# Moving the gate products ahead of their table piece, and three edits beside it, in the expert stage of a two-block transformer kernel

## The reference, cut to what matters

```python
def peer_ffn(h, w_q, sub_keys, u_tab, v_tab):
    q = (hf @ w_q).reshape(T, PEER_HEADS, 2, PEER_HALF)
    s = jnp.einsum('thpd,hpnd->thpn', q, sub_keys)          # 8 heads, 2 sides, 128 keys
    sv, si = lax.top_k(s, PEER_TOPK)                        # the best 16 of each side
    cand = sv[:, :, 0, :, None] + sv[:, :, 1, None, :]
    cv, ci = lax.top_k(cand.reshape(...), PEER_TOPK)        # the best 16 of 256 sums
    expert = ...                                            # first key * 128 + second key
    g = jax.nn.softmax(cv, axis=-1)
    ...
        a = gelu(einsum('cd,chkd->chk', x_c, u_tab[e_c]))
        return einsum('chk,chkd->cd', g_c * a, v_tab[e_c])
```

## Time and profile before

| What | Value |
|---|---|
| median of 3 runs | 1623.45 us (1622.08 to 1624.24) |
| the profiled execution | 1628.74 us, its span 1626.9 us |
| mean granted clock of PE | 0.987 |
| PE busy | 1551.1 us (95%) |
| PEld busy | 1339.1 us (82%) |
| DVE busy | 1132.8 us (70%) |
| ACT busy | 812.6 us (50%) |

### The profile page before, as it was taken

One profiled execution on the slowest core, in us unless ns is written; L12 is line 12 of the kernel. 1 busy time (PEld: TensorE's weight loads), 2 busy tenths in 40 slices (PEclk: granted clock), 3 DMA queues, 4 the chain that ended last, 5 costly groups with the idle time before them and its releaser, 6 DMA issues.

```text
span 1626.9 us, 30962 instructions
## 1 busy us (share of the span) xinstructions
PE 1551.1 (95%) x10658; PEld 1339.1 (82%) x10658; DVE 1132.8 (70%) x2580; ACT 812.6 (50%) x1362; POOL 105.9 (7%) x132
## 2 busy tenths in 40 slices
PE   6999999999999989998999999999999999999997
PEld 5877877896777768776999999999998777778886
DVE  3565666646666475448469996888888999965555
ACT  3664565446457545444356665344334444445454
POOL 1030600100113100000000000000000000000000
PEclk9999999999999999989999999999999999999999
DMA  6443654666355556424544546444444444465552
GB/s 240 153 167 125 214 188 135 218 192 235 129 189 181 205 177 233 149 73 168 188 136 168 182 166 207 155 156 160 159 156 151 160 167 162 161 209 192 192 193 103
DMA packets 78215, 280.40 MB, mean 172 GB/s; under 512 B 9377, under 2 KB 11457, under 8 KB 76865
## 3 DMA queue, kind: packets, MB, share of 16 engines
q1 hardware_dynamic: 74176, 261.97, 48.0%
q0 software_dynamic: 3968, 17.52, 3.2%
HBM read 277.31 MB, written 2.14 MB: 172 GB/s over the span
## 4 chain that ended last, share of the span: by engine, by line
PE 78%; DVE 15%; ACT 3%; issue 2%; DMA 2%; POOL 0%; ACTq 0%; DVEq 0%; POOLq 0%
PE banks L714 22%; PE banks L715 21%; PE banks L716 21%; DVE w_lo L1526 5%; PE banks L1137 3%; PE banks L901 2%; PE banks L860 2%; PE banks L799 2%; PE banks L821 1%; PE banks L911 1%; PE banks L910 1%; DMA arena<-x_spill 1%; ACT w_hi L1213 1%; DVE arena L2009 1%; PE banks L909 1%
## 5 line engine op out<-in xcount | busy, mean ns | idle before, releaser
L1526 DVE TENSOR_TENSOR w_lo<-raw,w_hi 128x1024 fp32r<-128x1024 f32 x456 | 549.9, 1210 | 307.8 <-ACT w_hi L1213 303.6
L1213 ACT ACTIVATE w_hi<-raw 128x1024 fp32r<-128x1024 f32 x456 | 474.3, 1043 | 572.2 <-PE banks L716 543.8
L714 PE MATMUL banks<-w_hi,xT_hi 128*128 128x512 f32 (+2 forms) x1140 | 453.4, 398 | 17.7 <-DVE w_lo L1526 10.7
L716 PE MATMUL banks<-w_hi,xT_lo 128*128 128x512 f32 (+2 forms) x1140 | 442.6, 388 | 0.0
L715 PE MATMUL banks<-w_lo,xT_hi 128*128 128x512 f32 (+2 forms) x1140 | 442.2, 388 | 0.0
L714 PE MATMUL banks<-xT_hi,w_hi 128*128 128x256 f32 x1360 | 391.8, 288 | 4.4 <-DVE w_lo L1526 1.7
L715 PE MATMUL banks<-xT_lo,w_hi 128*128 128x256 f32 x1360 | 385.9, 284 | 0.0
L716 PE MATMUL banks<-xT_hi,w_lo 128*128 128x256 f32 x1360 | 385.7, 284 | 0.0
L714 PEld LDWEIGHTS banks<-w_hi,xT_hi 128*128 128x128 f32 x1140 | 216.7, 190 | 64.7 <-issue 8.9
L714 PEld LDWEIGHTS banks<-xT_hi,w_hi 128*128 128x128 f32 x1360 | 261.2, 192 | 5.8 <-issue 3.8
L715 PEld LDWEIGHTS banks<-xT_lo,w_hi 128*128 128x128 f32 x1360 | 261.7, 192 | 0.1
(11 more groups left out here) (204 smaller groups left out, 1345.1 us busy)
## 6 DMA issues: line engine op xcount, KB each, us to landing
raw<-stream SPq DMA_DIRECT2D x490, 512.0 KB, 3.6
arena<-ln_in POOLq DMA_DIRECT2D x4, 1024.0 KB, 6.2
arena<-x_spill POOLq DMA_DIRECT2D x3, 1024.0 KB, 10.4
arena<-mod_rows POOLq DMA_DIRECT2D x2, 1536.0 KB, 9.6
raw<-stream SPq DMA_DIRECT2D x6, 256.0 KB, 4.5
arena<-g_in POOLq DMA_DIRECT2D x3, 512.0 KB, 11.1
raw<-stream SPq DMA_DIRECT2D x8, 160.0 KB, 2.4
arena<-bands_in POOLq DMA_DIRECT2D x1, 1024.0 KB, 6.1
```

What stands on the lines that cost most here:

```text
L714: pe.matmul(out, stationary[0], moving[0], start=first, stop=False, **k)
L716: return pe.matmul(out, stationary[1], moving[0], start=False, stop=last, **k)
L1213: act.activation(part(w_hi[:, s]), part(half_raw(s)), ACT.Copy).then_inc(piece_hi, 1)
L1526: dve.tensor_tensor(part(w_lo[:, s]), part(half_raw(s)), part(w_hi[:, s].bitcast(F32)), ALU.subtract).then_inc(piece_lo, 1)
```

## The change

Five edits, all in the expert part.

1. On PE, `gates` stands ahead of the piece's product in each step of loops 2 and 3. The steps of DVE keep their order.
2. The one-hot rows of a loop's first step are made ahead of the loop: those of loop 2 ahead of DVE's wait for `a_taken`, those of loop 3 ahead of the last `gate_hidden` of loop 2. The refills of ring slot 3 at both loop ends move behind the splits of the first four rows.
3. The rows of `hidden`'s second half are split into slots 4 to 7 of `xT_hi` and `xT_lo`, which were free in loop 3, in place of slots 0 to 3.
4. The matmuls that clear banks 0 to 3 wait one by one for `a_taken`, in place of all of them for the last.
5. The scores' units take the bank pairs 0, 2, 3, 1. Each waits for its own unit of the queries, and loop 1 waits for the first unit's copies; ACT lets PE into banks 2 and 3 only when all scores are copied (`a_taken` is raised by 2, and by 2 more behind the wait).

```diff
-        E["scores"] = [Unit(plan, "own", [...] , COPY2) for j in range(4)]
+        E["scores"] = [Unit(plan, "own", [...] , COPY2,
+                            pair=(0, 2, 3, 1)[j]) for j in range(4)]
...
-            wait_put(pe, E["q"])
             pe.wait_ge(keys_loaded, 16)
             for j4, u in enumerate(E["scores"]):
+                wait_put(pe, E["q"][j4:j4 + 1])
                 bank_free(u)
...
-            def second_table(j, s):
+            def second_table(j, s, row=0):
...
-            wait_put(pe, E["scores"])
+            wait_put(pe, E["scores"][:1])
...
             with pe.Fori(0, HALF // RING) as i:
                 for s in range(RING):
+                    gates(RING * i, s)
                     first_table(RING * i + HALF, s)
-                    gates(RING * i, s)
-
-            pe.wait_ge(a_taken, NKEYS + RING)
+
             for q in range(4):
+                pe.wait_ge(a_taken, NKEYS + q + 1)
                 pe.matmul(banks[:, q], const("zeros").bitcast(BF16)[:, 0:P], kept[:, 0:2 * P].bitcast(BF16), start=True, stop=True)
             with pe.Fori(0, HALF // RING) as i:
                 for s in range(RING):
+                    gates(RING * i + HALF, s)
                     second_table(RING * i, s)
-                    gates(RING * i + HALF, s)
             with pe.Fori(0, HALF // RING - 1) as i:
                 for s in range(RING):
-                    second_table(RING * i + HALF, s)
+                    second_table(RING * i + HALF, s, RING)
...
-            act.sem_inc(a_taken, RING)
+            act.sem_inc(a_taken, 2)
+            wait_put(act, E["scores"])
+            act.sem_inc(a_taken, RING - 2)
...
-            with act.Fori(0, HALF // RING) as i:
+            with act.Fori(0, HALF // RING - 1) as i:
                 for s in range(RING):
                     gelu(RING * i + HALF, s)
-
+            for s in range(RING - 1):
+                gelu(NKEYS - RING, s)
+            act.wait_ge(piece_used, FIRST_U + NKEYS)
+            gelu_only(NKEYS - RING, RING - 1)
             act.wait_ge(g_taken, HALF + 2)
             for s in range(RING):
                 split_hidden(0, s)
+            split_piece(FIRST_U + NKEYS, RING - 1)
...
-            for s in range(RING):
+            for s in range(RING - 1):
                 refill(HALF - RING, s, True, False)
 
             act.wait_ge(g_taken, 2 * HALF + 2)
             for s in range(RING):
-                split_hidden(HALF, s)
+                split_hidden(HALF, s, RING)
+            refill(HALF - RING, RING - 1, True, False)
...
-                one_hot(half, 0, 0)
                 with dve.Fori(0, HALF // RING - 1) as i:
                     for s in range(RING):
                         step(i, s, True, rows)
-                for s in range(RING):
-                    step(HALF // RING - 1, s, s < RING - 1, False)
+                for s in range(RING - 1):
+                    step(HALF // RING - 1, s, True, False)
+                if half == 0:
+                    one_hot(1, 0, 0)
+                gate_hidden(half, HALF - RING, RING - 1)
...
+            one_hot(0, 0, 0)
             dve.wait_ge(a_taken, HALF + RING)
             gate_half(0, FIRST_U + HALF, False)
             dve.wait_ge(a_taken, NKEYS + RING)
             for s in range(RING):
                 rest_of_hidden(0, s)
+            rest_of_piece(FIRST_U + NKEYS, RING - 1)
             gate_half(1, FIRST_V, True)
             for s in range(RING):
-                rest_of_hidden(HALF, s)
+                rest_of_hidden(HALF, s, RING)
+            rest_of_piece(FIRST_V + HALF, RING - 1)
```

More of the change, by code:

```diff
@@ L428, in build @@
         E["q"] = feature_units(peer["qT"], 2 * PEER_HEADS)
-        E["scores"] = [Unit(plan, "own", [peer["scores"][:, b, 4 * j:4 * j + 4] for b in range(B)], COPY2) for j in range(4)]
+        E["scores"] = [Unit(plan, "own", [peer["scores"][:, b, 4 * j:4 * j + 4] for b in range(B)], COPY2,
+                            pair=(0, 2, 3, 1)[j]) for j in range(4)]
         E["pick"] = [Unit(plan, "turn", [picked[:, 0:2], picked[:, 2:3]], [("act", "copy"), ("dve", "three_parts")], tiles=3, pair=3)]
@@ L1146, in second_table @@
                     for d in range(D // COLS):
-                        mm = parts_product(banks[:, 2 * b + d], [x[:, s, b * P:(b + 1) * P] for x in (xT_hi, xT_lo)],
+                        mm = parts_product(banks[:, 2 * b + d], [x[:, row + s, b * P:(b + 1) * P] for x in (xT_hi, xT_lo)],
                                            [x[:, s, d * COLS:(d + 1) * COLS] for x in (w_hi, w_lo)],
@@ L1175, in _ @@
                 for s in range(RING):
+                    gates(RING * i + HALF, s)
                     second_table(RING * i, s)
-                    gates(RING * i + HALF, s)
             with pe.Fori(0, HALF // RING - 1) as i:
                 for s in range(RING):
-                    second_table(RING * i + HALF, s)
+                    second_table(RING * i + HALF, s, RING)
             def last_products(b, d, s):
-                return parts_product(banks[:, 2 * b + d], [x[:, s, b * P:(b + 1) * P] for x in (xT_hi, xT_lo)],
+                return parts_product(banks[:, 2 * b + d], [x[:, RING + s, b * P:(b + 1) * P] for x in (xT_hi, xT_lo)],
                                      [x[:, s, d * COLS:(d + 1) * COLS] for x in (w_hi, w_lo)], False, False, skip_group_check=True)
@@ L1432, in _, with gelu_only @@
                 evacuate(u)
+            def gelu_only(j, s):
+                act.activation(hidden[:, bass.ds(j + s, 1)].rearrange("p a t -> p (a t)"), banks[:, s, 0:S],
+                               ACT.Gelu).then_inc(a_taken, 1)
             def gelu(j, s):
@@ L1437, in gelu, with split_hidden, refill @@
                 split_piece(FIRST_U + j + RING, s)
[L1438 to L1445, removed]
+                gelu_only(j, s)
+            def split_hidden(j, s, row=0):
+                act.activation(xT_hi[:, row + s], hidden[:, bass.ds(j + s, 1)].rearrange("p a t -> p (a t)"), ACT.Copy).then_inc(hidden_hi, 1)
+            def refill(j, s, pieces, rows, row=0):
                 act.wait_ge(piece_used, FIRST_V + j + s + 1)
@@ L1449, in refill @@
                 if rows:
-                    split_hidden(j + RING, s)
-            act.sem_inc(a_taken, RING)
+                    split_hidden(j + RING, s, row)
+            act.sem_inc(a_taken, 2)
+            wait_put(act, E["scores"])
+            act.sem_inc(a_taken, RING - 2)
             act.wait_ge(spilled, 16)
@@ L1483, in _ @@
             for s in range(RING):
-                split_hidden(HALF, s)
+                split_hidden(HALF, s, RING)
+            refill(HALF - RING, RING - 1, True, False)
             with act.Fori(0, HALF // RING - 1) as i:
                 for s in range(RING):
-                    refill(RING * i + HALF, s, True, True)
+                    refill(RING * i + HALF, s, True, True, RING)
             root_table()
@@ L2083, in rest_of_piece, with rest_of_hidden @@
                 split_rest(s)
-            def rest_of_hidden(j, s):
+            def rest_of_hidden(j, s, row=0):
                 dve.wait_ge(hidden_hi, j + s + 1)
-                dve.tensor_tensor(xT_lo[:, s], hidden[:, bass.ds(j + s, 1)].rearrange("p a t -> p (a t)"), xT_hi[:, s].bitcast(F32),
-                                  ALU.subtract).then_inc(hidden_lo, 1)
+                dve.tensor_tensor(xT_lo[:, row + s], hidden[:, bass.ds(j + s, 1)].rearrange("p a t -> p (a t)"),
+                                  xT_hi[:, row + s].bitcast(F32), ALU.subtract).then_inc(hidden_lo, 1)
             def gate_half(half, first_piece, rows):
@@ L2120, in _ @@
                     rest_of_piece(FIRST_V + HALF + RING * i + RING, s)
-                    rest_of_hidden(RING * i + HALF + RING, s)
+                    rest_of_hidden(RING * i + HALF + RING, s, RING)
             dve.wait_ge(end_loaded, 48)
```

## The result

| | before | after |
|---|---|---|
| median | 1623.85 us (4 runs) | 1664.24 us (1663.61 to 1665.28, 4 runs) |
| profiled execution: span | 1626.9 us | 1662.7 us |
| ratio of the times | | 1.0246, 95% interval 1.0234 to 1.0258 |

A forecast was written before the change was run, and what follows sets the result against it. PE was taken to bound the kernel, 78% of the span, without waits inside loops 2 and 3. Terms 18.5 + 22.9 - 2.0 - 1.3 = +38.1 us took the median from 1623.45 to 1661.5, range 1652 to 1671.

The forecast's parts named there:

- loop 2, first gates to end of last piece: Loop 2: late one-hot rows, branches and low clock at its start make it 228.5 us, before 210.00: +18.5.
- joint and loop 3, to loop 4: From loop 2's end to loop 4's first product: 234.0 us for 211.1, with late one-hot rows: +22.9.
- clock and rest behind loop 4's start: Loop 4's start: the 2.36 us idle goes, and the low clock behind it too: -2.0.
- scores: Around the scores: the 1.18 us wait goes, with the issue around it: -1.3, bounds -2.5 and 0.
- The chain in the steps: Loops 2 and 3: gates s+2 start at least 3.71 or 4.05 us after piece s is issued, 0.38 or 0.84 late.
- the branches: Loop 2: ACT starts a piece 0.1 us later in one step of four, at its loop's branch; 1.4 us added.
- the formula: Two steps take 3.71 + 3.33 us (7.04) in loop 2 and 4.05 + 3.21 us (7.26) in loop 3.
- Loop 2's start: First gates come at the same time as before, PE idles 4.0 us ahead of them, low clock costs 2.2 us.
- The joints: Loop 3's first product at about 1.8 us, its next gates another 1.1 us late; no wait at loop 4.
- the rows are not late: Rival for loops 2 and 3: one-hot rows 0.38 and 0.84 us sooner; 1622.8, or 1615.5 with first rows; chance 0.07.
- A clock that falls in the loops: Second rival, loops 2 and 3: one step in four at half clock, +80, some 1740 us; chance 0.03.
- A price per restart: Third rival, late gates in the loops: 0.1 us for each of 62, +6, 1668 us; chance 0.16.

The follow-up runs named there:

- e1: Changed kernel with VectorE's step reordered: gate_hidden, then the one-hot rows for the gates two steps on, then rest_of_piece; 1624.7 us, ratio 0.9998.
- e5: Changed kernel with one more VectorE instruction (128x512 bf16, output unread) in each one_hot; 1686.10 us, ratio 1.0382.
- e6: Changed kernel with one more VectorE instruction (128x512 bf16, output unread) per step, between gate_hidden and rest_of_piece; 1665.29 us, ratio 1.0257.
- e3: Changed kernel with the gates behind the piece again in loop 3 alone; 1637.69 us, ratio 1.0080.
- e4: Changed kernel with the second half's rows of hidden split into slots 0 to 3 again; 1665.37 us, ratio 1.0250.
- e2: e1 plus loop 2's one-hot rows of steps 0 and 1 made right behind the picks and each half's last gate_hidden ahead of the last rest_of_piece; 1616.35 us.
- e7: Kernel before the change with one more VectorE instruction (128x512 bf16, output unread) in each one_hot; 1628.99 us, ratio 1.0030.
- e9: e2 with the gates behind the piece in loops 2 and 3, as in the kernel before; 1622.82 us, ratio 0.9983.

## Why the prediction was right, point by point

| Term | forecast | measured, from the two traces |
|---|---|---|
| loop 2, first gates to end of last piece | 228.5 against 210.00: +18.5 | 228.37: +18.4 |
| of this, low clock at the start | 2.2 | 5.50 - 3.33 = 2.2 |
| joint and loop 3, to loop 4 | 234.0 against 211.1: +22.9 | 234.58: +23.5 |
| clock and rest behind loop 4's start | -2.0 | 183.35 against 184.96: -1.6 |
| scores | -1.3 | 7.49 against 8.56: -1.1 |
| sum | +38.1 | +39.2 |

The spans differ by 35.8 us only, since the profiled execution of before had its scores at 820.87 and that of after at 817.52, ahead of all that was changed; the medians differ by 40.4. Between 39.2 and 40.4 lies 0.07% of the time, which I can't place. The forecast for the median, 1661.5, took over the 5.3 us by which the profiled execution of before was longer than its median. That step had no ground: the profiled execution of after is 0.3 us longer than its median, 1664.53 against 1664.24. So the sum of the terms was 1.1 us short, and the forecast of the median 2.7.

**The chain in the steps** held in its mechanism (e1, e5, e6) and its size: 7.04 us and 1.4 for the branches make 7.085 for a mean pair of loop 2, and 7.08 is there; in loop 3 7.26 were forecast and 7.27 are there. The branches show in loop 2 as one late step in four of 3.80 us and not 3.71. The share between the two loops held too (e3). One detail did not hold throughout: the wait was to fall on each second step. In loop 2 it does. In loop 3 it moves: steps of 3.49 and 3.78 us at 1301.05 to 1308.32, both longer than 3.21, but 3.23 and 4.14 at 1450.78 to 1458.15. By the formula a pair's sum is fixed, and its share between the two steps is free as long as neither is above 4.05, or 4.14 with a branch.

**Loop 2's start** went as worked out: the first gates came 191.39 us after loop 1's start, 191.40 before, and 3.99 us of idle stood ahead of them, with the clock low behind.

**The joints.** First product of loop 3: at 1.7 us and not 1.8 (1244.77 to 1246.45), and the gates behind its piece (2.87 us) 0.87 us late (1250.19) and not 1.1. At loop 4 I wrote that nothing is waited for; there are 0.44 us. The last `gate_hidden` stands behind a `rest_of_piece` on DVE, the same kind of dependence that I had followed in the loops and did not follow here. That joint and loop 3 together are within 0.6 us of the forecast is in part luck: the first joint was 0.3 us shorter than forecast, and loop 4's start 0.6 later. The gain was credited to two edits together; e4 shows that one of them carries none of it.

**The rivals.** That the rows are not late was given 0.07 and a condition; e1 and e2 make the condition true by another edit, and give 1624.7 and 1616.4 where it had 1622.8 and 1615.5. A clock that falls in the loops did not come: 0.99 for loop 2, whose start holds all of it, and 1.00 for loop 3 with some 9% of idle time. A price per restart is not seen: two steps take what the chain alone gives.

## What to carry to other kernels

Where one engine's queue holds both what the next step needs and what waits for this step, moving the consumer one place forward takes a whole step from the slack; here 2.96 us to spare in loop 2 (6.67 - 3.71) became 0.38 us too late. Follow the chain from the event that frees the waiting instruction to the consumer's new place, and compare it with one step. An instruction costs by where it stands in the queue and not by what it takes: the same 0.34 us of VectorE cost 22 us on the chain and about nothing beside it. When a reordering loses, look for the producer that must be moved with it; here an earlier place of the one-hot rows on VectorE, in the steps and at the loops' ends (e1, e2), turned a loss of 2.5% into a kernel 0.45% faster than the one before.

## What the runs showed of the hardware

At the joints of the expert part TensorE's granted clock was full behind idle times of 1.03, 1.12, 1.18 and 1.42 us. It went to its lower level behind those of 1.84 (e7), 1.98 and 2.26 (e9), 2.36 (before) and 3.99 us (after). I had not expected it behind 1.98. What this costs is not fixed: behind 3.99 us the first step of loop 2 took 5.50 us in the changed kernel and 4.66 in e4, for 3.33 at the full clock. Nor does the length of one idle time decide it. In the first part of the changed kernel's trace an idle of 2.07 us left the clock full, and one of 1.12 us, where PE works in short groups, was followed by the lower level:

```profile
62.99 0.47 PE L715 MATMUL banks<-w_hi,xT_hi 128*128 128x512 f32 x1 [2.07 <-DVE xT_lo L1571]
...
60.00:66.00 6.00, 3.93 (x22) 3.23 (x21) 3.78 (x7) 3.00 (x7) 0.00 (x0) 1.00 0.54 177
...
693.53 1.46 PE L861 MATMUL banks<-arena 64*128 64x128 f32 x4 [1.12 <-issue]
...
693.70:700.50 6.80, 6.80 (x22) 5.11 (x22) 2.44 (x11) 2.27 (x10) 0.00 (x0) 0.50 0.24 78
```

What does decide it is not shown here. The short waits in the loops did not lower it: loop 3 of the changed kernel has 36 in its 64 steps, of up to 0.8 us, and a granted clock of 1.00. By the rule of the Trainium skill weighed in the prediction (TensorE: Matmul & The Clock Gate, "A second HAM failure mode: psum-queue depth-cycling") such waits make the clock swing; the trace of this kernel disagrees.
